# A decoder step on one core: the low halves of the projection weights by an accumulating DMA, with heads, buffers and queues reordered

## What is computed

```python
z = rmsnorm(x, g_mix) @ w_in            # columns: u | va | q | k | v | gate_a | gate_b
a = gelu(u) * (tril(w_s) @ rmsnorm(gelu(va)) + b_s)
q, k = rotary(rmsnorm(q) * g_q), rotary(rmsnorm(k) * g_k)     # 24 heads of 64, in 3 groups
b = attention(q, k, v)                  # window 129 keys at distance 1, 4, 16; prompt and cache
x = x + (sigmoid(gate_a) * (a @ w_oa) + sigmoid(gate_b) * (b @ w_ob)) @ w_o
x = x + relu(rmsnorm(x) @ w_ff1) ** 2 @ w_ff2
x = x + sigmoid(rmsnorm(x) @ w_ple_gate) * (p @ w_ple_proj)
```

## Time and profile before

| | |
|---|---|
| three runs | 1139.98, 1140.40, 1140.81 us; median 1140.4 |
| the profiled execution, its own time | 1141.28 us |
| its span, first to last instruction | 1139.9 us |
| mean granted TensorE clock | 0.965 of full speed |
| TensorE busy | 94% of the span |
| bytes moved by DMA | 196.17 MB, mean 172 GB/s |
| slots 0 to 59 (natural panels) | up to about 410 us |
| feed-forward and the last projection | from about 690 us |

### The profile page before, as it was taken

One profiled execution on the slowest core, in us unless ns is written; L12 is line 12 of the kernel. 1 busy time (PEld: TensorE's weight loads), 2 busy tenths in 40 slices (PEclk: granted clock), 3 DMA queues, 4 the chain that ended last, 5 costly groups with the idle time before them and its releaser, 6 DMA issues.

```text
span 1139.9 us, 21051 instructions
## 1 busy us (share of the span) xinstructions
PE 1073.9 (94%) x8508; PEld 1058.3 (93%) x8508; DVE 708.8 (62%) x917; ACT 430.8 (38%) x737; POOL 263.4 (23%) x374
## 2 busy tenths in 40 slices
PE   8999889898799789899989999999999999999997
PEld 8998879897799789899989999999999999999996
DVE  6679678886679677897947335443443444444552
ACT  5431544544531546325226444311421331233331
POOL 2541233113322000727810111100100101102300
PEclk9999899999799889989989999999999999999999
DMA  6647554677458645557673234565565554654422
GB/s 197 204 129 245 168 159 148 200 219 218 133 154 265 206 150 176 164 163 213 190 232 112 78 108 156 168 196 180 174 203 172 192 191 157 209 186 157 162 69 79
DMA packets 130958, 196.17 MB, mean 172 GB/s; under 512 B 32080, under 2 KB 108144, under 8 KB 129088
## 3 DMA queue, kind: packets, MB, share of 16 engines
q1 hardware_dynamic: 106448, 123.54, 34.8%
q0 software_dynamic: 10304, 63.28, 17.1%
q10 hardware_dynamic: 14128, 8.26, 2.4%
HBM read 186.07 MB, written 62.00 MB: 218 GB/s over the span
## 4 chain that ended last, share of the span: by engine, by line
PE 66%; DVE 10%; DMA 8%; POOL 5%; issue 4%; ACT 4%; SPq 2%; ACTq 0%; DVEq 0%; POOLq 0%
PE gm L1058 54%; DMA w_raw<-in_w_in 4%; PE gm L1034 2%; DVE kv L1453 2%; PE gm L1035 2%; PE gm L1036 2%; POOL kv L1824 2%; POOL st L1863 2%; POOL st L1793 1%; ACT prob L904 1%; DMA out_kvp<-fin 1%; DMA out_kvp<-V 1%; SPq L505 1%; ACT w_hi L614 1%; PE psS L1212 1%
## 5 line engine op out<-in xcount | busy, mean ns | idle before, releaser
L1058 PE MATMUL gm<-h_hi,w_hi 128*128 128x272 f32 x1088 | 230.6, 293 | 3.9 <-DVE z L1398 3.0
L1058 PE MATMUL gm<-h_hi,w_lo 128*128 128x272 f32 x1088 | 227.0, 290 | 0.0
L1058 PE MATMUL gm<-h_lo,w_hi 128*128 128x272 f32 x1088 | 226.5, 290 | 0.0
L614 ACT CAST w_hi<-w_raw 128x1024 fp32r<-128x1024 f32 x150 | 150.9, 1047 | 173.9 <-PE gm L1058 116.5
L1335 DVE TENSOR_TENSOR w_lo<-w_raw,w_hi 128x1024 fp32r<-128x1024 f32 x150 | 178.0, 1224 | 47.2 <-ACT w_hi L614 45.4
L1034 PE MATMUL gm<-w_hi,h_hi 128*128 128x256 f32 x640 | 191.5, 299 | 5.6 <-issue 5.6
L1035 PE MATMUL gm<-w_hi,h_lo 128*128 128x256 f32 x640 | 184.5, 288 | 0.0
L1036 PE MATMUL gm<-w_lo,h_hi 128*128 128x256 f32 x640 | 183.8, 287 | 0.0
L1058 PEld LDWEIGHTS gm<-h_hi,w_hi 128*128 128x128 f32 x1088 | 172.9, 191 | 5.1 <-issue 4.6
L1058 PEld LDWEIGHTS gm<-h_lo,w_hi 128*128 128x128 f32 x1088 | 173.2, 191 | 0.0
L1058 PEld LDWEIGHTS gm<-h_hi,w_lo 128*128 128x128 f32 x1088 | 171.9, 191 | 0.0
(11 more groups left out here) (256 smaller groups left out, 1509.1 us busy)
## 6 DMA issues: line engine op xcount, KB each, us to landing
w_raw<-in_w_ff SPq DMA_DIRECT2D x64, 512.0 KB, 5.1
out_kvs<-in_cache_kv_w POOLq DMA_DIRECT2D x64, 510.0 KB, 4.1
w_raw<-in_w_in SPq DMA_DIRECT2D x60, 512.0 KB, 7.3
kv<-in_cache_kv_w SPq DMA_DIRECT2D x128, 128.0 KB
kv<-in_cache_kv_w SPq DMA_DIRECT2D x64, 256.0 KB
out_kvs<-in_cache_kv_w POOLq DMA_DIRECT2D x32, 508.0 KB, 4.7
kv<-in_cache_kv_w POOLq DMA_DIRECT2D x128, 64.0 KB, 4.0
w_raw<-in_w_o SPq DMA_DIRECT2D x8, 512.0 KB, 4.4
```

Of the source, the lines that this page charges most:

```text
L614: nc.scalar.copy(w_hi[:, r, hh * 1024:(hh + 1) * 1024], w_raw[:, hh]).then_inc(w_hi_done, 1)
L1058: last = nc.tensor.matmul(gm[:, 2 * b2 + half, 0:HALF], w, x[:, k0 + k, half * HALF:(half + 1) * HALF], start=first, stop=end)
```

## The change

- `ADDED` are panels 2 to 20, 19 panels: those whose predecessor is natural. For them ScalarE, after `w_hi`, also writes `w_lo = -w_hi` in two halves, and POOL then issues two DMAs of 512 KB that load the weights from HBM again and add them into `w_lo`. TensorE waits for these (`w_added`). VectorE's `split_lo` is left out for them.
- `load_panel` waits for `w_hi_done` of the panel before where that is in `ADDED`.
- Heads have three buffers: `fin[sub]` and a new `fs` for the samples, at partitions 32 to 63, with st, rot and cs at the same partitions. The division by 64 goes into the square's scale, so POOL only adds EPS before the power.
- VectorE: a sample unit's `scale_heads` comes after the next unit's sum, rotation and maxima; where `split_lo` stays in a natural slot, it comes after that; in the second unit of a q or k panel the first chunk comes ahead of `scale_heads`.
- ScalarE: `square_samples` and `store_sample_heads` come ahead of `split_hi`.
- The chunks have a new string: 68 instead of 60 before slot 60, group 2's last key in slot 70 (was 79), the last chunk in slot 81 (was 84).
- The 16 DMAs O0<-O_blk go to POOL, four each in slots 38 to 41. The combination moves from slots 67 and 69 to 72, 73 and 74.

```diff
+ADDED = [_p for _p in range(2, P_FF) if PANELS[_p - 1][0] in NATURAL]
...
-CHUNKS_IN_SLOT = ("000000000002203112002102012102212213002103003002112111"
-                  "103113122110000001131100121213200000000000")
+CHUNKS_IN_SLOT = ("000000000001212212102201102202212322102202102101211212"
+                  "203213121110010111010100121200000000000000")
...
+        fs = sb("fs", [128, 256], F32, A_K - 1024)[NS:2 * NS]
...
@@ load_panel (SP)
-                    if not (isinstance(pp, int) and pp == 0):
-                        sp.wait_ge(w_lo_done, 2 * (pp - 1) + hh + 1)
+                    if isinstance(pp, int) and pp - 1 in ADDED:
+                        sp.wait_ge(w_hi_done, 2 * (pp - 1) + hh + 1)
+                    elif not (isinstance(pp, int) and pp == 0):
+                        sp.wait_ge(w_lo_done, split_count(pp - 1) + (hh - 1))
...
-                if s == 40:
-                    sp.wait_ge(o_out, 16)
-                    for a in range(4):
-                        for b in range(4):
-                            sp.dma_start(O0[32 * b:32 * b + 32, a], O_blk[a:128:4, b]).then_inc(o_moved, 16)
...
@@ split_hi (ScalarE), behind the two copies
+                if isinstance(pp, int) and pp in ADDED:
+                    for hh in range(2):
+                        act.wait_ge(w_hi_done, 2 * pp + hh + 1)
+                        cols = slice(hh * 1024, hh * 1024 + 1024)
+                        nc.scalar.mul(w_lo[:, r, cols], w_hi[:, r, cols].bitcast(F32), -1.0).then_inc(w_negated, 1)
...
@@ slots (ScalarE)
+                if s >= 1 and UNITS[s - 1][4] == 2 and UNITS[s - 1][1] in ("k", "q", "va"):
+                    square_samples(s - 1)
+                if s >= 2 and UNITS[s - 2][1] in ("k", "q") and UNITS[s - 2][4] == 2:
+                    store_sample_heads(s - 2)
                 if sub == 0:
                     split_hi(p + 1, (p + 1) % 2, panel_end(p - 1) if p >= 1 else None)
...
@@ unit (TensorE)
                     pe.wait_ge(w_hi_done, 2 * (p + 1))
-                    pe.wait_ge(w_lo_done, 2 * (p + 1))
+                    if p in ADDED:
+                        pe.wait_ge(w_added[p % 2], 32 * (ADDED.index(p) // 2 + 1))
+                    else:
+                        pe.wait_ge(w_lo_done, split_count(p))
...
@@ rotate_heads (VectorE)
-                if n >= 2:
-                    prev = [x for x in range(u) if UNITS[x][1] in ("k", "q") and kqn(x) == n - 2][0]
+                if n >= 3:
+                    prev = [x for x in range(u) if UNITS[x][1] in ("k", "q") and kqn(x) == n - 3][0]
...
@@ slots (VectorE)
                 if tail:
                     sum_squares(s - 1)
-                if sub == 0:
+                if sub == 0 and kind not in NATURAL:
                     split_lo(p + 1, (p + 1) % 2)
-                if tail:
-                    scale_heads(s - 1)
...
                 for job in SJOBS.get(s, []):
                     take_scores(job)
-                if kind in ("k", "q") and sub < 2:
-                    scale_heads(s)
+                if tail:
+                    scale_heads(s - 1)
+                if sub == 0 and kind in NATURAL and p + 1 not in ADDED:
+                    split_lo(p + 1, (p + 1) % 2)
...
+                first = CH_AT.get(s, [])[:1] if kind in ("k", "q") and sub == 1 else []
+                for n in first:
+                    (take_keys if CHUNKS[n][0] == "keys" else take_values)(n)
+                if kind in ("k", "q") and sub < 2:
+                    scale_heads(s)
+                for n in CH_AT.get(s, [])[len(first):]:
...
@@ slots (POOL)
+                if sub == 0 and p + 1 in ADDED:
+                    x, r = ADDED.index(p + 1), (p + 1) % 2
+                    for hh in range(2):
+                        pool.wait_ge(w_negated, 2 * x + hh + 1)
+                        nk = 1024 // COLS.get(PANELS[p + 1][0], 256)
+                        pool.dma_start(w_lo[:, r, hh * 1024:(hh + 1) * 1024].rearrange("p (k n) -> p k n", k=nk),
+                                       wview(p + 1, hh).bitcast(F32R), accum_op=ALU.add).then_inc(w_added[r], 16)
                 if kind in ("k", "q"):
...
-                    link(gp.tensor_scalar(v, v, 1.0 / HD, EPS, ALU.mult, ALU.add))
-                    inverse_root(v).then_inc(rstd_ready, 1)
+                    link(gp.tensor_scalar(v, v, EPS, None, ALU.add))
+                    gp.tensor_tensor(v, v, mhalf[at, 0:4 * nt], ALU.pow).then_inc(rstd_ready, 1)
...
+                if 38 <= s < 42:
+                    a = s - 38
+                    pool.wait_ge(o_out, 16)
+                    for b in range(4):
+                        pool.dma_start(O0[32 * b:32 * b + 32, a], O_blk[a:128:4, b]).then_inc(o_moved, 16)
```

More of the change, by code:

```diff
@@ L93, in stores_heads, with split_count @@
     return sub == 2 or (kind == "k" and not (g == 0 and sub == 0))
+ADDED = [_p for _p in range(2, P_FF) if PANELS[_p - 1][0] in NATURAL]
+def split_count(pp):
+    if isinstance(pp, int) and pp < P_FF:
+        return 2 * sum(1 for x in range(pp + 1) if x not in ADDED)
+    return 2 * pp + (2 - 2 * len(ADDED))
 PIECES = [(0, 2 * c + x, b) for c in range(H // 2) for b in range(2) for x in range(2)] + [(1, h, 0) for h in range(H)] + [(2, h, 0) for h in range(H)]
@@ L448, in build @@
         V_STORES = [16 * 2, 16 * 8, 16 * 8]
-        FIN_STORES = [0, 0]
+        FIN_STORES = [0, 0, 0]
         for u in range(U_FF):
             if UNITS[u][1] in ("k", "q") and stores_heads(u):
-                FIN_STORES[kqn(u) % 2] += 16
+                FIN_STORES[kqn(u) % 3] += 16
         def fin_count(n):
-            return sum(16 for u in range(U_FF) if UNITS[u][1] in ("k", "q") and stores_heads(u) and kqn(u) <= n and kqn(u) % 2 == n % 2)
+            return sum(16 for u in range(U_FF) if UNITS[u][1] in ("k", "q") and stores_heads(u) and kqn(u) <= n and kqn(u) % 3 == n % 3)
         def wait_heads(engine, kind, g):
@@ L461, in wait_heads @@
                 n = kqn(UNIT[kind, (g, i, 2)])
-                engine.wait_ge(fin_stored[n % 2], fin_count(n))
+                engine.wait_ge(fin_stored[n % 3], fin_count(n))
         def s_bank(j):
@@ L588, in _ @@
             sp.wait_ge(cache_copied, 16 * (64 + 32 + 16))
-            sp.wait_ge(fin_stored[0], FIN_STORES[0])
-            sp.wait_ge(fin_stored[1], FIN_STORES[1])
+            for x in range(3):
+                sp.wait_ge(fin_stored[x], FIN_STORES[x])
             for g in range(NG):
@@ L749, in take_transposes @@
                         act.wait_ge(fin_ready, kqn(u) + 1)
-                        f = fin[:, kqn(u) % 2]
+                        f = fin[:, sub]
                         cols = slice(256 * i, 256 * i + 256)
-                        done = fin_stored[kqn(u) % 2]
+                        done = fin_stored[sub]
                         if g == 0:
@@ L881, in _ @@
                     gained_hi(0, sub, zc(UNIT["wo", sub]))
-                if s >= 2 and UNITS[s - 2][1] in ("k", "q") and UNITS[s - 2][4] == 2:
-                    store_sample_heads(s - 2)
                 for job in TJOBS.get(s, []):
@@ L1289, in hidden_group @@
                     pe.wait_ge(w_hi_done, 2 * (pp + 1))
-                    pe.wait_ge(w_lo_done, 2 * (pp + 1))
+                    pe.wait_ge(w_lo_done, split_count(pp))
                     for sub in range(2):
@@ L1940, in constants @@
     for a in range(5):
-        rows = np.arange(128 if a < 4 else NS)
+        rows = np.arange(128)
         pos = (128 * a + rows if a < 4 else WIN[2] + rows % T).astype(np.float32)
```

51 lines of the change are left out of this document (29 added, 22 removed).

## The result

The changed kernel takes 1223.6 us in the median (1221.5 to 1225.1, four runs), beside 1140.2 us of the kernel before on the same chip: ratio 1.0733, 95% interval 1.0711 to 1.0755. It is 83 us slower, where 1118 us (1097 to 1156) had been forecast. The profiled execution took 1225.1 us at a span of 1223.5.

A forecast was written before the change was run, and what follows sets the result against it. TensorE, 94% busy, was taken as the bound, its waits priced at 1.7 times their length for the chain through VectorE; 1141.3 less 43.7 gains plus 21 late landings, less 0.9 for the median, gave 1118 us (1097 to 1156).

The forecast's parts named there:

- The accumulating transfer: At panel starts, w_lo lands 8 us after the second negation, costing 21 us together; bounds 0 and 90.
- The room: In early panels, 5.6 us are left between the negation's end, 8.5 us in, and the next panel's start.
- The late landings: First matmuls wait for w_lo: 13 us in panels 2 to 6, 8 us in later ones, together 21 us.
- the own range: Whole kernel, main forecast: 1102 to 1134 us, varying the exponentials' wait and late landings from 8 to 28 us.
- Rival A: First matmuls of panels 2 to 20: slow accumulation, 1150 us at 11 us, 1173 us at 13 us; chance 0.27.
- The exponentials: TensorE's 20.8 us wait for ScalarE's exponentials, priced at 35.4 us, halves through relief of VectorE: 17.7 us gained.
- rival B: Attention chain: ScalarE takes VectorE's place, so gains of 17.7 and 3.5 us don't come: 1139 us; chance 0.14.
- The late w_lo at panel starts: First matmuls' 5.6 us wait, read as w_lo_done, goes if the new transfer comes in time: 9.5 us gained.
- the loads on `w_hi_done` and from SP's block: Earlier weight requests and SP losing 14.03 us of issues shorten mask waits: 8 us gained, bounds 0 and 12.
- Chunks earlier: Group-2 keys end at slot 70 instead of 79, so the sum awaited at slot 84 is early: 5 us gained.
- The third head buffer: Takes half of TensorE's wait for rotated heads, 7 us as priced: 3.5 us gained, bounds 0 and 7.
- sample heads: POOL's twelve small scalings, no longer beside VectorE's difference, fall from 2.24 to 0.5 to 1 us; no VectorE wait behind them.

The follow-up runs named there:

- h1: The changed kernel with the 38 accumulating transfers left out, TensorE waiting for ScalarE's negation only: 1125.1 us, 0.9877 of the kernel before.
- e1: The changed kernel with no accumulating panels, VectorE forming every low half again, all reorderings kept: 1126.9 us, 0.9875 of the kernel before.
- h2: The change without accumulation, VectorE's difference at its old place, old chunk table, the 16 block transfers back on SP: 1119.5 us, 0.9812.
- f4: The kernel before with nothing but the new table of chunks: 1148.1 us, 1.0079 of the kernel before.
- h3: The change without accumulation, difference at its old place, old chunk table, VectorE's and ScalarE's order as before: 1137.7 us, 0.9972.
- f2: The changed kernel without accumulation, VectorE's difference back at its old place behind the sample sums: 1124.6 us, 0.9878.
- g2: The changed kernel with plain copies instead of accumulating transfers and chunk loads from the sixth on thinned: 1139.2 us, 1.0018.

## Why the prediction was wrong

The whole, in measured steps: 1139.7 (before, beside h1) less 14.6 for all that the change does with a free transfer, to 1125.1, plus 98.5 for the transfers, to 1223.6. The forecast had 43.7 and 21.

*The accumulating transfer: the step that failed.* "0.6 + 2 + 6.4 us after the first negation, 8 us after the second" was right where little else ran: 8.1, 9.0 and 8.4 us. The price of two passes came out as well, whatever the packet really does. The transfers' engine time on the page is (0.262 x 1223.5 - 0.176 x 1129.6) = 121.8 us of all 16 engines, against e1, for 19.9 MB: 6.1 us per MB for the forecast's 6.4, and 1.9 times the 3.2 of SP's queue. What failed is that a time for a quiet queue was put into panels that have none. The chunk loads, the raw weights and the window copies were in that stretch already, at a share of 0.60, and the forecast said of the added 0.25 that it "lengthens loads; covered by their earlier issue". It lengthened the transfer itself, to 10 to 24 us in 16 of 19 panels, and that transfer has no cover: it starts late in a panel and TensorE needs it at the next one's start. The upper bound of 15 us added 2.8 us for traffic, from the median landing of the w_in loads; nine panels lie over it, the worst at 23.6 us. Half of the engines for each of two busy queues would have given 2 x 6.4 = 13 us, close to the measured median of 14.8, but not the six worst: the queues take turns by packet, and in the worst stretch the accumulation had 22% of the engines while others had no work.

*The room.* 5.6 us were counted as left after the negation, from the earlier trace rows. They were rows of a kernel that doesn't stall. The stalled matmul comes ahead of transposes that ScalarE takes before its copy, so a late panel makes the next one late: 10.5 us into the panel, not 8.5. The issue on POOL took 1.44 us and not 0.6 to 0.75; the second half goes that much later. The late landings, 21 us, were also entered at their length, though every other wait of TensorE was priced at 1.7 times its own; and the own range's lower end doesn't follow from its terms, which at their best give some 1091 and not 1102 us.

*Rival A* named the mechanism, "the engines at 0.85 make a queue"; its break-even of 10 us was passed and its condition "12 or more, with the granted clock below 1 before 101 us" came true for most: 14 of 19 panels landed 12 us or more after their first issue, and the clock was 0.88. But it was priced at 1150 to 1173 us and cut off at 1156. The cost splits up in this way: against h1 the idle time of TensorE rose by 83.4 us (142.9 - 59.5) and its busy time by 17.5 (1080.6 - 1063.1), the 100.9 us by which the spans differ. An idle us more cost 1.2 us here, not 1.7. These stalls are longer than those that the 1.7 was taken from, 6.4 us in the mean; whether that is the reason, no run tests.

*The exponentials: rival B was right.* Half the wait, 17.7 us, was to go. With a free transfer none of it does (21.9 us in h1), and ScalarE's 38 passes eat 13.6 of the 15.3 us that leaving out VectorE's 38 brings. That h1 still took 1125.1 us and not B's 1139 is about what the order of the work brings (below), which B didn't have either. That the row is gone in the changed kernel shows only that the stalls at panel starts cover it. The forecast took half of the wait off for ScalarE's longer block; it should have taken all.

*The other terms.* The late w_lo at panel starts (9.5 us) and the loads on `w_hi_done` and from SP's block (8 us): the row of 5.6 us is gone in h1, where no transfer is waited for, but the 14 us block was covered (h2), ScalarE stands for raw weights 52.1 us in h1 against 56.9 before, and the waits for masks, from which the 8 us were taken, are 11.3 us in h1 against 7.1. "Chunks earlier", 5 us, was wrong in sign for the table alone: its wait of 2.9 us is gone in f4, but the waits for exponentials rise to 28.4 us. The third head buffer, 3.5 us, brings together with the shorter scaling and the blocks on POOL no more than the 2 us between h3 and before. Not in the sum at all was the order of VectorE's and ScalarE's work, which brings the 14 us: the edit was noted under "sample heads" and valued only for the scaling on POOL. That small scaling fell as forecast, to 0.23 us from 2.24:

```profile
L1905 POOL TENSOR_SCALAR st<-st 32x4 f32<-32x4 f32 x12 | 2.7, 225 | 126.5 <-DVE st L1374 126.5
...
L1891 POOL TENSOR_SCALAR st<-st 32x4 f32<-32x4 f32 x12 | 2.3, 188 | 190.2 <-DVE st L1368 190.2
...
L1903 POOL TENSOR_SCALAR st<-st 32x4 f32<-32x4 f32 x12 | 11.9, 995 | 81.1 <-DVE st L1374 81.1
```

The change both shortened this scaling and took the difference away from beside it. The second row, of the accumulation alone, has the old scaling without the difference: 0.19 us. The third, of f2, has the new scaling with the difference beside it: 1.0 us. So it is the difference that made it slow.

*The page of the skill.* The estimate by the Trainium skill, "DMA: Bandwidth & Descriptors", section "Anatomy of one DMA — SWDGE (gpsimd) path", was 3.2 us a half. The shortest accumulation took 5.9 us, the shortest plain one in these kernels' quiet panels 5.1, or 4.1 with thinned chunks. The measurement decides: a kernel can't be planned by that figure where descriptors are 1 KB and other queues work.

What stays open: whether the second pass of a packet is a read of SBUF, whether chunk loads spread over all 16 engines would let the accumulation through (no run has them), and what of the 14 us between g2 (1139.2) and h1 (1125.1) is the plain transfer's latency and what its share of the engines.

## What to carry to other kernels

A transfer on the critical path is priced at the share of the DMA engines that it will get beside what runs there (by packets, and small packets beside large ones get less), not at its time when alone; where its start can't move ahead of that traffic, an engine that does the same in 2.4 us is cheaper. Before work is moved from one engine to another, ask whether both are links of the same chain: then the move gives back what it takes, as 15.3 and 13.6 us here. And leave the expensive part of an idea out once, whatever the output: the run with free transfers showed that the idea had nothing measurable to win here even at its best.

## What the runs showed of the hardware

- An accumulating transfer between DRAM and SBUF used 1.9 times the engine time of SP's plain loads per byte: 6.1 against 3.2 us of all 16 engines per MB. A packet of 1 KB took 105 ns in the mean (101 at least), against 57 (44) on SP's queue in the same stretch; copied instead of added, 81 ns (60) on POOL's queue.
- Its issue on POOL took 1.44 us for 512 KB, the same transfer without the addition 0.76 us.
- Two queues with work took turns by packet, whatever is urgent: 182 and 181 packets in 5 us, but 22.3% and 32.9% of the engines, for 1 KB packets against mostly 4 KB ones. Two transfers can be late together while the engines are only 56% busy.
- POOL's 32x4 scaling takes 0.19 us, not 2.24, without a VectorE difference beside it (0.23 against 1.0 us in its shorter form). That is the rule of the Trainium skill, "SBUF — State Buffer", section "Who interferes with whom". The gain is larger than forecast, which had 0.5 to 1 us left.
